# Loading each weight unit as two halves, in a float32 two-block transformer kernel

## The reference: what is computed

```python
for l in range(2):
    shift, scale, gate = split(silu(c) @ w_mod[l] + b_mod[l], 3)       # and the same for the context
    hx = rmsnorm(x, norm_g[l]) * (1 + scale) + shift                   # hc for the context, 256 tokens
    q, k, v, g_att, u_pool, g_pool, a_conv, b_conv, g_conv = split(hx @ w_in[l])     # 2048 -> 6656
    y = concat(diff_attention * silu(g_att), pool * silu(g_pool), conv * silu(g_conv)) @ w_out[l]
    x = x + gate * y                                                   # layer 0 updates the context too
```

## Time and profile before

| what | value |
|---|---|
| median of 3 runs | 3117.34 us (3112.94 to 3127.66) |
| the profiled execution | 3121.88 us |
| its span, first to last instruction | 3120.1 us |
| PE (matmul) busy | 2952.9 us, 95% |
| PEld (weight load) busy | 2532.5 us, 81% |
| POOL busy | 1809.5 us, 58% |
| VectorE (DVE) busy | 1696.7 us, 54% |
| ACT busy | 1441.2 us, 46% |
| moved from HBM | 615.44 MB, 198 GB/s over the span |
| mean granted TensorE clock | 0.977 |

### The profile page before, as it was taken

How to read it: one execution, slowest core, us unless ns; L and a number is a source line. 1 busy time by engine, 2 the same in 40 slices (tenths; PEclk the granted TensorE clock), 3 DMA queues, 4 the chain that set the end, 5 groups by cost and what they waited for, 6 DMA issues and landing times.

```text
span 3120.1 us, 50669 instructions
## 1 busy us (share of the span) xinstructions
PE 2952.9 (95%) x19441; PEld 2532.5 (81%) x19441; DVE 1696.7 (54%) x2723; ACT 1441.2 (46%) x2239; POOL 1809.5 (58%) x756
## 2 busy tenths in 40 slices
PE   6899999999899989999978999999998999999998
PEld 4688886777687978888767988899987888888887
DVE  2487973555423769158578786673625555553000
ACT  3222223566322522268546675575445555554333
POOL 1244443322333654455656555667786888888887
PEclk9899999999899999999988999999999999999999
DMA  9766322111665793233765775444554666655555
GB/s 371 313 256 273 143 96 81 68 68 62 260 253 213 306 396 123 83 124 122 282 230 208 263 265 205 144 151 160 176 202 166 238 229 234 225 200 183 194 190 186
DMA packets 89739, 619.50 MB, mean 199 GB/s; under 512 B 9936, under 2 KB 11264, under 8 KB 18304
## 3 DMA queue, kind: packets, MB, share of 16 engines
q1 hardware_dynamic: 88448, 612.36, 53.2%
q10 hardware_dynamic: 1152, 5.24, 0.5%
HBM read 615.44 MB, written 2.12 MB: 198 GB/s over the span
## 4 chain that ended last, share of the span: by engine, by line
issue 58%; POOL 41%; POOLq 1%; PE 0%; DVE 0%; DVEq 0%
POOL w_low L666 41%; POOLq L661 1%; POOLq L665 0%; POOLq L666 0%; PE bank L701 0%; PE bank L702 0%; DVE region L1853 0%; DVE region L1856 0%; DVEq L1853 0%; POOLq L2642 0%
## 5 line engine op out<-in xcount | busy, mean ns | idle before, releaser
L666 POOL TENSOR_TENSOR w_low<-raw,w_high 128x1024 fp32r<-128x1024 f32 x752 | 1809.3, 2424 | 1303.8 <-ACT w_high L1208 1301.9
L1208 ACT ACTIVATE w_high<-raw 128x1024 fp32r<-128x1024 f32 x752 | 783.1, 1055 | 976.6 <-PE bank L714 382.8
L712 PE MATMUL bank<-h,w_high 128*128 128x256 f32 (+1 forms) x2816 | 955.2, 339 | 18.7 <-POOL w_low L666 17.3
L713 PE MATMUL bank<-h,w_high 128*128 128x256 f32 (+1 forms) x2816 | 937.1, 333 | 0.0
L714 PE MATMUL bank<-h,w_low 128*128 128x256 f32 (+1 forms) x2816 | 937.0, 333 | 0.0
L712 PEld LDWEIGHTS bank<-h,w_high 128*128 128x128 f32 x2816 | 539.5, 192 | 99.4 <-issue 25.3
L701 PE MATMUL bank<-h,w_high 128*128 128x512 f32 x1664 | 594.7, 402 | 12.6 <-POOL w_low L666 8.1
L713 PEld LDWEIGHTS bank<-h,w_high 128*128 128x128 f32 x2816 | 539.7, 192 | 50.2 <-issue 0.7
L714 PEld LDWEIGHTS bank<-h,w_low 128*128 128x128 f32 x2816 | 538.9, 191 | 51.0
L702 PE MATMUL bank<-h,w_low 128*128 128x256 f32 x1664 | 468.4, 281 | 0.0
L701 PEld LDWEIGHTS bank<-h,w_high 128*128 128x128 f32 x1664 | 315.3, 190 | 96.7 <-POOL w_low L666 16.2
(11 more groups left out here) (256 smaller groups left out, 3494.4 us busy)
## 6 DMA issues: line engine op xcount, KB each, us to landing
raw<-in_w_in SPq DMA_DIRECT2D x172, 1024.0 KB, 4.8
raw<-in_w_up SPq DMA_DIRECT2D x88, 1024.0 KB, 4.7
region<-in_w_mods SPq DMA_DIRECT2D x76, 1024.0 KB, 6.1
region<-in_w_rows SPq DMA_DIRECT2D x55, 1024.0 KB, 7.9
raw<-in_w_out SPq DMA_DIRECT2D x48, 1024.0 KB, 4.8
raw<-in_w_down SPq DMA_DIRECT2D x48, 1024.0 KB, 4.7
row_extra<-in_w_rows SPq DMA_DIRECT2D x41, 1024.0 KB, 7.0
row_extra<-in_w_half_rows SPq DMA_DIRECT2D x22, 512.0 KB, 5.1
```

The lines of the kernel that those rows point to most:

```text
L666: nc.gpsimd.tensor_tensor(WL[s][:, part], RAW[s][:, part], WH[s][:, part], ALU.subtract) \
L712: nc.tensor.matmul(bank[:, 0:n], WH[slot][:, w], h, start=first and j == 0, stop=False)
L713: nc.tensor.matmul(bank[:, 0:n], WH[slot][:, w], l, start=False, stop=False)
L1208: return nc.scalar.activation(out, in_, func, **kw)
```

## The change

The load of a unit becomes two loads of 1024 columns (0.5 MB) each. Each has a semaphore of its own, so there are four `raw_in` semaphores in place of two. Each waits for the split of its own half of the unit two before; up to now the whole load waited for both. `high` waits for the semaphore of its half. The two products that read `RAW` directly wait for both. Three semaphores of the attention that each layer had for itself (`_tr`, `_pv`, `_nb`) become one each for both layers, with 32 counted for the first.

```diff
-    raw_in = [sem("raw_in0"), sem("raw_in1")]
+    raw_in = [[sem(f"raw_in{slot}{half}") for half in "ab"] for slot in range(2)]
...
+        def raw_half(slot, half, weights):
+
+            part = slice(HALF * half, HALF * (half + 1))
+            sp.dma_start(RAW[slot][:, part], weights[:, part]).then_inc(raw_in[slot][half], 16)
+
         def first_unit(n):
-            if n >= 2:
-                sp.wait_ge(split_ready, 2 * (n - 2) + 2)
-            sp.dma_start(RAW[n % 2][:], dram["w_in0"][n]).then_inc(raw_in[n % 2], 16)
+            for half in range(2):
+                if n >= 2:
+                    sp.wait_ge(split_ready, 2 * (n - 2) + half + 1)
+                raw_half(n % 2, half, dram["w_in0"][n])
...
             def two(i):
                 for s in range(2):
-                    sp.wait_ge(split_ready, 2 * (u0 - 1) + 4 * i + 2 * s)
-                    sp.dma_start(RAW[s][:], w[ds(first // 2 + i, 1), s].rearrange("a p n -> (a p) n")) \
-                        .then_inc(raw_in[s], 16)
+                    weights = w[ds(first // 2 + i, 1), s].rearrange("a p n -> (a p) n")
+                    for half in range(2):
+                        sp.wait_ge(split_ready, 2 * (u0 - 1) + 4 * i + 2 * s - 1 + half)
+                        raw_half(s, half, weights)
...
             def one(n):
-                sp.wait_ge(split_ready, 2 * (u0 + n - 1))
-                sp.dma_start(RAW[n % 2][:], dram[name][n]).then_inc(raw_in[n % 2], 16)
+                for half in range(2):
+                    sp.wait_ge(split_ready, 2 * (u0 + n - 1) - 1 + half)
+                    raw_half(n % 2, half, dram[name][n])
...
-            pe.wait_ge(raw_in[u % 2], 16 * (u // 2 + 1))
+            for half in range(2):
+                pe.wait_ge(raw_in[u % 2][half], 16 * (u // 2 + 1))
...
-            act.wait_ge(raw_in[slot], 16 * (u // 2 + 1) + 8 * per * i)
+            act.wait_ge(raw_in[slot][half], 16 * (u // 2 + 1) + 8 * per * i)
...
-                act.wait_ge(sem(nm + "_nb"), g + 1)
+                act.wait_ge(sem("at_nb"), 32 * l + g + 1)
```

More of the change, by code:

```diff
@@ L546, in two @@
                 for s in range(2):
-                    sp.wait_ge(split_ready, 2 * (u0 - 1) + 4 * i + 2 * s)
-                    sp.dma_start(RAW[s][:], w[ds(first // 2 + i, 1), s].rearrange("a p n -> (a p) n")) \
-                        .then_inc(raw_in[s], 16)
+                    weights = w[ds(first // 2 + i, 1), s].rearrange("a p n -> (a p) n")
+                    for half in range(2):
+                        sp.wait_ge(split_ready, 2 * (u0 - 1) + 4 * i + 2 * s - 1 + half)
+                        raw_half(s, half, weights)
             def unit(i, t):
-                sp.wait_ge(split_ready, 2 * (u0 - 1) + 2 * t + 8 * i)
-                sp.dma_start(RAW[t % 2][:], w[ds(first // 2 + t // 2 + 2 * i, 1), t % 2].rearrange("a p n -> (a p) n")) \
-                    .then_inc(raw_in[t % 2], 16)
+                weights = w[ds(first // 2 + t // 2 + 2 * i, 1), t % 2].rearrange("a p n -> (a p) n")
+                for half in range(2):
+                    sp.wait_ge(split_ready, 2 * (u0 - 1) + 2 * t + 8 * i - 1 + half)
+                    raw_half(t % 2, half, weights)
             def one(n):
-                sp.wait_ge(split_ready, 2 * (u0 + n - 1))
-                sp.dma_start(RAW[n % 2][:], dram[name][n]).then_inc(raw_in[n % 2], 16)
+                for half in range(2):
+                    sp.wait_ge(split_ready, 2 * (u0 + n - 1) - 1 + half)
+                    raw_half(n % 2, half, dram[name][n])
             if name in ("w_in0", "w_in1"):
@@ L638, in _ @@
                         mod_load(BUF_SSM[b], b, M_SSM + t)
-                    sp.wait_ge(split_ready, 2 * (u + 8 + t) + 2)
-                    sp.dma_start(RAW[t % 2][:], w[10 + t]).then_inc(raw_in[t % 2], 16)
+                    for half in range(2):
+                        sp.wait_ge(split_ready, 2 * (u + 8 + t) + 1 + half)
+                        raw_half(t % 2, half, w[10 + t])
                     j = t // 4
@@ L908, in attention @@
                     last = nc.tensor.transpose(BANK[6][:, P * c:P * (c + 1)], PP[g % 2][0][:, P * c:P * (c + 1)], IDENT)
-                last.then_inc(sem(nm + "_tr"), 1)
+                last.then_inc(sem("at_tr"), 1)
                 if g + 2 < steps:
@@ L939, in attention @@
                                             v[:, h, P * c:P * (c + 1)], start=c == 0, stop=c == nk // P - 1)
-                last.then_inc(sem(nm + "_pv"), 1)
+                last.then_inc(sem("at_pv"), 1)
             pe.wait_ge(sem(nm + "_exp"), steps)
@@ L1326, in head_squares @@
             def head_squares(h):
-                act.wait_ge(sem(nm + "_pv"), J * (h + 1))
+                act.wait_ge(sem("at_pv"), 32 * l + J * (h + 1))
                 if h:
@@ L1386, in attention @@
                 h, s, nk = g // J, g % J, jobs[g % J][1]
-                act.wait_ge(sem(nm + "_tr"), g + 1)
+                act.wait_ge(sem("at_tr"), 32 * l + g + 1)
                 run(AT[g % 2][:, 0:nk], BANK[6][:, 0:nk], ACT.Copy).then_inc(sem(nm + "_at"), 1)
@@ L2081, in maxima @@
                 V.tensor_scalar(NB[:, 2 * b:2 * b + 2], MX[:, 2 * b:2 * b + 2], -0.125, None, ALU.mult) \
-                    .then_inc(sem(nm + "_nb"), 1)
+                    .then_inc(sem("at_nb"), 1)
             def head(h):
```

## The result

| what | before | changed |
|---|---|---|
| median | 3119.98 us (4 runs, 3112.94 to 3127.66) | 3086.12 us (4 runs, 3074.62 to 3095.54) |
| ratio of the two | | 0.9889 [0.9848, 0.9931] |
| profiled execution | 3121.88 us | 3095.54 us |
| its span | 3120.1 us | 3093.8 us |

The kernel is 33.9 us faster by the medians and 26.3 us by the two profiled executions; 27.1 were forecast. That spread is as large as the gain, and part of the experiments went into it.

A forecast was written before the change was run, and what follows sets the result against it. It took TensorE, busy 95%, as the bound, with its waits for POOL's low part as the loss. Terms 17.7 + 5.5 + 2.2 + 0 + 1.2 + 1.5 - 1 = 27.1 us; forecast 3090 us, 8 in 10 from 3078 to 3104.

The forecast's parts named there:

- The circle of w_down: In `w_down`, request, landing, copy and two low halves take 10.85 us for two units, against 10.3 that TensorE takes.
- The term of w_down, 17.7 us: In `w_down`, PEld's waits for POOL hold 18.0 us of loss, of which 17.7 go; bounds 11 and 19.
- The landing, 3.5 us: In `w_down`, a half load lands in about 3.5 us; bounds 3.3 and 5.7.
- The rival of serial halves: Halves come one behind the other, 7.0 us per unit; `w_down` and `w_up` grow, +175 us, about 3292; 3%.
- The term of w_up, 5.5 us: In `w_up`, 5.5 of the 6.4 us that TensorE waits go; bounds 2 and 6.4.
- the 4 to 6 us named as a sign: In `w_up`, the wait for POOL falls below 2 us and the stage gets 4 to 6 us shorter.
- The row-load stages and the two short stretches, 4.9 us in all: Shorter waits for POOL: 2.2 us in `w_out1`, 0 and 1.2 in `w_in1`, 1.5 in two short stretches.
- The long wait of w_in1, 0: In `w_in1`, the 10.2 us wait stays, as ACT's copy waits for VectorE's "h"; 0 counted, bounds -2 and +3.
- the rival in which it shrinks: Rows land earlier, `w_in1`'s 10.2 us wait loses 3, short waits go whole (+5): 35 us gained, 3082; 10%.
- POOL as the next bound: POOL, busy 94% of `w_down`, decides from 2.57 us per half; at 2.65 some 14 us gained in all, 3103; 9%.
- The second push, 1 us: Added load instructions on SPq delay rows between 1034 and 1172 us; 1 us lost, at most 7.6.
- the rival in which `w_in1` gives most of the gain back: Rows for VectorE are pushed, `w_in1`'s 10.2 us wait grows by 7.6; 20 us gained remain, 3097; 8%.

The follow-up runs named there:

- e1_tail: Half loads in `w_up` and `w_down` only, whole loads in all stages before, against the changed kernel; 3098.98 us, ratio 0.9928 to the kernel before.
- e2_head: Half loads in all stages up to `w_out2`, whole loads in `w_up` and `w_down`, against the changed kernel; 3106.26 us, ratio 0.9946 to the kernel before.
- e3_late: Changed kernel, but both halves asked for only when both halves of the unit two before are split; 3102.47 us, ratio 0.9937 to the kernel before.
- e4_joint: Changed kernel with its early requests, but ACT's copies wait until both halves have landed; 3111.38 us, ratio 0.9967 to the kernel before.
- e9_rows_whole: Changed kernel with every second block's products turned round, plus whole loads in `w_in1` and `w_out1`; 3089.19 us, 10.8 us above the same without those whole loads.
- a1_same: The changed kernel run once more with no edit, as the measure for its group of runs; 3088.51 us, ratio 0.9889 to the kernel before.
- e8_order_old: The kernel before, whole loads, with only the product order of every second block turned round (512, 256, 256, 512); 3127.61 us, ratio 1.0003 to the kernel before.

## Why the prediction was right, and where its terms were off

**The circle of w_down: right.** Load, copy and two low halves in one circle set the stage; the halves break it, TensorE becomes the bound and PEld's waits go (28 to none). e1_tail and e2_head place the gain in this stage. The prediction gave two causes at once, the earlier request and the shorter load; e3_late and e4_joint show that in `w_down` each alone does it, whole or nearly so.

**The term of w_down, 17.7 us: 14.7 or 19.4, by TensorE's pace.** The 18 us of waits went, as the term has it. With them gone, the stage is 704 blocks at a pace: at 0.3533 us, 248.7, and it took 253.4; at 0.3467, 244.1, and it took 248.7. The prediction took one pace (0.35) for both kernels, and missed that it moves: from the mean of 0.3493 before, 0.3533 costs 2.8 us over 704 blocks and 0.3467 gives 1.8, which is most of the difference to the term. The kernel before changes between the two at restarts; that its stalls went also took away the occasions to change. A reading beside it was wrong without harm: PEld does not idle 0.04 us between any two loads, only behind the one of the low weights; from 2984.28 to 2984.40 its loads overlap.

**The landing, 3.5 us: 4.3, no matter.** It is inside the 3.4 to 4.8 named, and even 5.7 would have done by the sum. That halves overlap is shown most directly by e3_late, where both are asked for within 0.52 us: half b has landed 4.6 us after its own request, 5.1 us after that of half a, and not 7.0 us. The rival of serial halves (+175 us) is out.

The rule against the change came from the Trainium skill ("DMA: Bandwidth & Descriptors", section "Measured (HBM→SBUF, 128 partitions, SWDGE, issued from GpSimd)"), which says to batch DMAs to 1 MiB or more to reach at least 75% of peak. That speaks of the share of peak bandwidth, for loads issued from GpSimd; these are issued from SyncE, and `w_down` moves 190 GB/s before and 198 after, far from the 423 of a full queue. So no run here tests the rule itself; what did not come is the loss that the prediction read into it.

The same page ("Anatomy of one DMA — SWDGE (gpsimd) path") says that most of the fixed part is waiting for the receipt of the write. The overlap in e3_late agrees with it, but does not show what the fixed part consists of.

**The term of w_up, 5.5 us: the waits went as forecast (7.3 to 1.2), the time did not.** Where the pace was 0.3533 the stage is shorter by 3.2 and 3.6 us, where it was 0.3467 by 12.4 and 11.9; the 4 to 6 us named as a sign came in neither. The kernel before had a mean of 0.3512: at 0.3533, 1408 blocks take 3.0 us more, which gives half of the 6 back, and at 0.3467 they take 6.3 less, which doubles it.

**The row-load stages and the two short stretches, 4.9 us in all: 4.8 in the first profile, up to 9.2 in the others.** PEld's waits ahead of `w_up` went from 26.7 to 21.9, 20.9, 20.5 and 17.5. By e9_rows_whole, `w_in1` and `w_out1` alone are worth 10.8. The term took only the earlier landing of the first half into account (1.24 us a wait); e3_late shows that the request 2.4 us earlier is needed there: without it the waits are 29.2 us, no better than before, and 8.3 above a1_same. e4_joint shows that it isn't enough: with it, but with a copy that waits for both halves, they are 34.9. With both parts they are 17.5 to 21.9 us in all eight such profiles, with a part missing or whole loads in these stages 25.6 to 34.9 in the other six. The likely reason is that a half asked for 2.4 us earlier gets its bytes ahead of row loads that are asked for behind it. The prediction had said that in one queue no half gets ahead of a row load that stood ahead of its unit; the trace bears that out (none of 613 loads of SyncE before landed ahead of one asked for earlier), but the prediction left out the row loads that stand behind the unit. That both parts are needed is shown, the reason is argued.

**The long wait of w_in1, 0: right.** 10.2 us before, 10.5 after, so the rival in which it shrinks is out, and the wait for VectorE behind it is there, in the changed kernel at 1085 to 1112 us:

```profile
ACT w_high L1220 <- DVE h L1831: 14.3, 1, 14.3
```

**POOL as the next bound: not reached.** A low half takes 2.402 us as before, and POOL is busy for 228.45 of 257 us, 89%. **The second push, 1 us: not seen as a loss.** `w_in1`, from POOL's first half in it to its first in `w_out1`, is 484.8 us against 486.4, and 134 to 832 us has its length within 1 us. So the rival in which `w_in1` gives most of the gain back is out too.

So the mechanism was right, but that the sum came within a microsecond, 27.1 against 26.3, was luck: its errors cancel. In the first profile `w_down` gave 14.7 us (3.0 less than its term), `w_up` 3.2 (2.3 less), and `w_up` began 8.3 us earlier, where the terms make 3.9. Of these 8.3, 4.8 are fewer waits of PEld; the rest is no more than what the start of the kernel alone differs by from one execution to the next, up to 9 us. Which stretch the rest of the medians' difference belongs to (33.9 against 26.3) isn't settled. The pace is the largest part that is known: the four profiled executions are 3095.54 and 3099.96 us at 0.3533, and 3079.33 and 3073.45 at 0.3467, and 2112 blocks times 0.0067 is 14 us of the difference. It also clouds the comparison of e1_tail and e3_late, whose profiled executions ran at 0.3533, with a median of the changed kernel that holds both.

## What to carry to other kernels

This is from one kernel. In a double buffer, add up the whole circle of a slot (request, landing, every step until the slot is free) and hold it against the consumer's time for two units; if it is longer, halve the grain, and let both the request and the first step go by halves, for a consumer that still waits for both halves can be worse off than with one load. Where other loads shared the queue both were needed (e3_late, e4_joint); where none did, either was nearly enough. The gain doesn't show in the length of a landing, which hardly fell. Once a stall is gone, the pace of the engine that is then the bound counts, and improving it first shows nothing (e8_order_old).

## What the runs showed of the hardware

- **TensorE had two steady paces for one stream of instructions.** Blocks of one product of 512 and one of 256 columns follow each other at 346.7 or at 353.3 ns, 832 or 848 cycles at 2.4 GHz, the higher clock level (granted clock 1.00 in `w_down`). The first two profiles of the changed kernel kept 353.3 through over 2000 blocks, the other two 346.7. In the nine profiles with this order it changed only at the border of two halves, where TensorE waits for `split_ready`, at times with hardly a stop: the shortest such step from block to block is 361 ns (e4_joint). Many restarts keep the pace; which one a restart picks was not found. With every second block turned round (512, 256, 256, 512) there is one pace, 696.6 ns for two blocks, with half loads and with whole ones.
- Products of one size showed no second pace: three of 512 columns take 680.0 ns (`w_in0`) and three of 256 take 360.0 ns (`w_abr`, `w_sbr`).
- **The length of a landing says little of what a load costs.** Half the bytes landed in 4.3 us in place of 4.7 in `w_down`, and in 6.9 in place of 5.1 in 1500 to 1600 us (`w_out1`), and TensorE waited less in both.
